# Norm sums and scale of the expert stage worked out in the first block's last weight tiles, and routes of one head with the first token block first

## What is computed

```
h   = rms_norm(x1, norm2_g) * (1 + scale2) + shift2            # 256 x 2048
q   = h @ peer_query            -> per head (8) two halves of 128
s   = q . peer_keys             -> per head and half 128 key scores
top = 16 best of each half; 16 x 16 pair sums; 16 best pairs   # expert = key_a * 128 + key_b
g   = softmax(16 best sums)
out = sum over 8 heads x 16 picks of
      g * gelu(peer_down[expert] . h) * peer_up[expert]        # rows of 2048
x2  = x1 + gt2 * out;  then rms_norm with final_g
```

## Time and profile before

| what | before |
|---|---|
| median of 3 runs | 3666.14 us |
| profiled execution, its own time | 3667.49 us |
| span of its trace | 3665.7 us |
| mean granted TensorE clock | 0.896 of 2.4 GHz |
| TensorE, VectorE, ScalarE, GpSimd busy | 2978.8, 1845.8, 1119.8, 2423.9 us |
| first block's last update ends, first gather, last gather issued at | 999.1, 1075.5, 2411.1 us |

### The profile page before, as it was taken

The page is one execution under the profiler, slowest core; times in us unless marked ns, Lnnn a source line. Parts: engine busy times, 40 slices in busy tenths (PEclk is TensorE's granted clock), DMA queues, the critical chain, the costliest instruction groups (busy, mean ns, idle before and its releaser), DMA issues. The chain is left out here.

```text
span 3665.7 us, 31629 instructions
## 1 busy us (share of the span) xinstructions
PE 2978.8 (81%) x11406; PEld 2100.8 (57%) x11406; DVE 1845.8 (50%) x2199; ACT 1119.8 (31%) x1784; POOL 2423.9 (66%) x1132
## 2 busy tenths in 40 slices
PE   6899999999876665555466676569999998999997
PEld 2677777888753432222122222238888877878876
DVE  1776365423146779998777667751147321121221
ACT  2422355344311111111121111124455444434433
POOL 0444575588724567766778778758767687888875
PEclk7999999999988887776778987779999998999998
DMA  9898643365548899999999999975545455556543
GB/s 390 295 362 314 226 158 121 115 199 191 185 168 362 368 419 427 427 427 427 422 427 427 425 427 425 427 282 184 174 148 185 138 184 183 189 191 201 191 155 142
DMA packets 314642, 1017.91 MB, mean 278 GB/s; under 512 B 21609, under 2 KB 24261, under 8 KB 246653
## 3 DMA queue, kind: packets, MB, share of 16 engines
q1 hardware_dynamic: 234032, 465.09, 36.9%
q0 software_dynamic: 73728, 536.90, 34.8%
q10 hardware_dynamic: 6732, 13.96, 1.2%
HBM read 1011.66 MB, written 4.23 MB: 277 GB/s over the span
## 5 line engine op out<-in xcount | busy, mean ns | idle before, releaser
L1638 PE MATMUL banks<-up_rows,pick_diagonal 128*128 128x512 f32 x1024 | 674.9, 820 | 496.1 <-DMA up_rows<-peer_up,picked_experts 465.4
L654 POOL TENSOR_TENSOR block_weights_lo<-weight_ring,block_weights_hi 128x1024 fp32r<-128x1024 f32 x224 | 552.8, 2478 | 421.4 <-ACT block_weights_hi L647 316.5
L1638 PEld LDWEIGHTS banks<-up_rows,pick_diagonal 128*128 128x128 f32 x1024 | 261.8, 268 | 887.5 <-issue 830.9
L1903 DVE CUSTOM_DVE_ANT_0 down_rows<-down_rows,h_tokens 128x2048 f32<-128x2048 f32 x256 | 585.0, 2291 | 243.9 <-DMA down_rows<-peer_down,picked_experts 235.8
L1565 POOL DMA_INDIRECT up_rows<-peer_up,picked_experts x256 | 472.0, 1844 | 319.8 <-PE banks L1638 165.1
L654 POOL TENSOR_TENSOR merge_weights_lo<-weight_ring,merge_weights_hi 128x1024 fp32r<-128x1024 f32 x208 | 500.4, 2408 | 123.0 <-ACT merge_weights_hi L647 122.9
L1559 POOL DMA_INDIRECT down_rows<-peer_down,picked_experts x256 | 468.2, 1829 | 165.0 <-DVE picked_experts L1843 86.6
L654 POOL TENSOR_TENSOR in_weights_lo<-weight_ring,in_weights_hi 128x1024 fp32r<-128x1024 f32 x176 | 423.6, 2416 | 136.0 <-ACT in_weights_hi L647 135.5
L647 ACT ACTIVATE block_weights_hi<-weight_ring 128x1024 fp32r<-128x1024 f32 x224 | 235.4, 1058 | 423.3 <-PE banks L512 225.4
L1733 ACT ACTIVATE pick_gelu<-pick_dots 128x2 f32<-128x2 f32 x128 | 26.0, 203 | 1067.1 <-DVE pick_dots L1903 1067.1
L1862 DVE SCALAR_TENSOR_TENSOR expert_sum<-up_rows,pick_share,expert_sum 128x2048 f32<-128x2048 f32 x125 | 293.9, 2351 | 79.1 <-ACT pick_share L1736 73.7
(11 more groups left out here) (477 smaller groups left out, 5033.0 us busy)
## 6 DMA issues: line engine op xcount, KB each, us to landing
weight_ring<-w_in SPq DMA_DIRECT2D x232, 1024.0 KB, 5.0
cond_ring<-w_ada SPq DMA_DIRECT2D x128, 512.0 KB, 6.4
weight_ring<-w_ada SPq DMA_DIRECT2D x32, 1024.0 KB, 9.0
weight_ring<-w_out SPq DMA_DIRECT2D x32, 1024.0 KB, 5.0
weight_ring<-peer_query SPq DMA_DIRECT2D x16, 1024.0 KB, 12.2
weight_ring<-w_ret_out SPq DMA_DIRECT2D x8, 1024.0 KB, 5.0
weight_ring<-w_mlstm_out SPq DMA_DIRECT2D x8, 1024.0 KB, 5.1
weight_ring<-w_mem_kv SPq DMA_DIRECT2D x8, 1024.0 KB, 16.1
```

What stands on the lines that cost most here:

```text
L654: pool.tensor_tensor(self.lo[:, at], ring.tile[:, slot, h * self.HALF:(h + 1) * self.HALF], self.hi[:, at], ALU.subtract).then_inc(ring.us ...
L1638: mm = pe.matmul(ps[:, 4 + b], diag[:, G % 2], up[:, p % ROWS, b * CG:(b + 1) * CG], start=(G % PER_TB == 0), stop=(G % PER_TB == PER_TB - ...
L1903: dve.tensor_tensor_reduce(down[:, p % ROWS], down[:, p % ROWS], h2[:, G // PER_TB], 1.0, 0.0, ALU.mult, ALU.add, dots[:, p:p + 1]).then_i ...
```

## The change

1. In the first block SyncE issues, after the tiles of the second `w_out` chunk, twelve loads: scale2 and norm2_g in four pieces each, the keys in two, shift2 in two, into columns of the block's own tensors that are no longer used; the small table is loaded at the block's start. VectorE forms (1 + scale2) * g in four pieces (`scales`) after the first token update, and multiplies the finished columns of x1 by it into `h2` (`scaled`), for chunks 0 to 2 after their update and for chunk 3 in `token_update`. ScalarE sums the squares of the finished columns (`token_squares`, two of 512 wide per chunk) into `e.ss2` and calls Sqrt once before the last of them. In the very last tile TensorE takes both halves for token block 0 before token block 1, and VectorE updates block 0 as soon as that half is done.
2. The expert stage starts with a reduce of `e.ss2`, variance, root and reciprocal. h of each token block is written in four pieces of 512 (times rstd, plus shift2), each with its own count, block 0 first. TensorE turns one fill of keys, block 0's four fills, then does queries and scores of key blocks 0 and 1 for token block 0 alone, then the other key fills and block 1, and so on: `UNITS` is the list of queries, the first four with one token block, the other fourteen (key blocks 2 to 15) with both. Five units are done ahead of the loop, unit 5 + G // 2 in it. The last use of a query chunk is at G = 0, 8, 16, the first of the next at G = 2, 10, 18. ScalarE has the exponential of route 0 between the copies of the keys and those of h of block 1.
3. A route is one head: 16 routes of 16 picks per token block and head, two key lists, one pair list, numbers and normalisation; each takes four groups (`PACE`). The picks of route r are needed at G = 8r.
4. GpSimd waits once for the turned keys before the first up gather.

The core of the diff:

```diff
                         sp.dma_start(x_again(n), tokens_of(io["x"][0])[:, :, n * CG:(n + 1) * CG]).then_inc(late_in, 16)
+                if c == W0 + 1:
+                    sp.wait_ge(m_turned, FILLS)
+                    for n in range(N_OUT):
+                        cols = slice(n * CG, (n + 1) * CG)
+                        sp.dma_start(scale2(n), e.mod_rows[0, 2 * D:3 * D][cols].partition_broadcast(P)).then_inc(early_in, 16)
+                        sp.dma_start(g2(n), io["norm2_g"][0, cols].partition_broadcast(P)).then_inc(early_in, 16)
+                    for j in range(2):
+                        sp.dma_start(early_keys(j), io["peer_keys"][0].rearrange("h a k d -> k (h a) d")[:, j * HP // 2:(j + 1) * HP // 2]).then_inc(early_in, 16)
+                        sp.dma_start(early_shift(j), e.mod_rows[0, D + j * D // 2:D + (j + 1) * D // 2].partition_broadcast(P)).then_inc(early_in, 16)
...
-                    for tb in range(TB):
-                        if first == 0 and h == 0 and g >= 2:
-                            if g - 2 < N_COLS:
...
+            def token_squares(n):
+                if n == 0:
+                    act.wait_ge(m_lo_out, FILLS)
+                for tb in range(TB):
+                    act.wait_ge(out_done, (2 * N_OUT + n) * TB + tb + 1)
+                    act.activation(ps[:, 4 + tb], e.x[:, tb, n * CG:(n + 1) * CG], ACT.Square, accum_out=e.ss2[:, tb, n:n + 1])
...
             def token_update(n):
                 g = Y0 + 2 * N_OUT + n
-                dve.wait_ge(split.free, split.free_after(M0 + tiles_at_end[g]))
                 for tb in range(TB):
+                    if n == N_OUT - 1 and tb == 0:
+                        dve.wait_ge(first_half_done, 1)
+                    else:
+                        dve.wait_ge(split.free, split.free_after(M0 + tiles_at_end[g]))
                     step(dve.tensor_tensor(prod[:, tb], ps[:, 2 * (g % 2) + tb], gt1(n), ALU.mult))
                     dve.tensor_tensor(e.x[:, tb, n * CG:(n + 1) * CG], x_again(n)[:, tb], prod[:, tb], ALU.add).then_inc(out_done, 1)
-                dve.wait_ge(out_done, (2 * N_OUT + n + 1) * TB)
+                    if n == N_OUT - 1:
+                        scaled(n, tb)
+
+            def scaled(n, tb):
+                dve.wait_ge(out_done, (2 * N_OUT + n) * TB + tb + 1)
+                cols = slice(n * CG, (n + 1) * CG)
+                step(dve.tensor_tensor(h2[:, tb, cols], e.x[:, tb, cols], scale2(n), ALU.mult))
+
+            def scales():
+                dve.wait_ge(early_in, 13 * 16)
+                for n in range(N_OUT):
+                    step(dve.scalar_tensor_tensor(scale2(n), scale2(n), 1.0, g2(n), ALU.add, ALU.mult))
...
-        PER_TB, PER_ROUTE = GROUPS // TB, NB // 2 * TOP // 2
-        ROUTES, R_PICKS = GROUPS // PER_ROUTE, NB // 2 * TOP
-        EARLY = 6
+        PER_TB, PER_ROUTE, PACE = GROUPS // TB, TOP // 2, 4
+        ROUTES, R_PICKS = GROUPS // PER_ROUTE, TOP
+        UNITS = [(i, (tb,)) for tb in range(TB) for i in range(2)] + [(i, (0, 1)) for i in range(2, HP)]
+        unit_of = lambda i, tb: 2 * tb + i if i < 2 else i + 2
+        q_count = lambda u: sum(1 for i, _ in UNITS[:u + 1] if i % NB < NB - 1)
+        EARLY = 5
...
+            turn_keys(0, 0)
+            for g in range(H_FILLS):
+                turn_h2(1 + g, 0, g)
+            pe.wait_ge(turned_out, 1 + H_FILLS)
+            for u in range(2):
+                query(u)
+            for u in range(2):
+                score(u)
+            for f in range(1, KEY_FILLS):
+                turn_keys(H_FILLS + f, f)
+            for g in range(H_FILLS):
+                turn_h2(KEYS_TURNED + g, 1, g)
             pe.wait_ge(turned_out, FILLS)
-            for i in range(EARLY):
-                query(i)
-                if 1 <= i < NB:
-                    score(i - 1)
-                if i == NB - 1:
-                    score(i)
-            score(EARLY - 2)
+            for u in range(2, 4):
+                query(u)
+            for u in range(2, 4):
+                score(u)
+            query(4)
+            score(4)
 
             for G in range(GROUPS):
                 p = 2 * G + 1
...
+            for u in range(2, 4):
+                copy_query(u)
+            for u in range(2, 4):
+                copy_score(u)
+            copy_query(4)
+            copy_score(4)
 
             for G in range(GROUPS):
                 first = 2 * G
@@ -1742,15 +1827,12 @@
                     act.wait_ge(odd_added, G - 1)
                 act.activation(diag[:, G % 2], e.ident[:], ACT.Copy, scale=share[:, first + 1:first + 2]).then_inc(diag_ready, 1)
 
-                if G == 0:
...
@@ -1882,18 +1959,17 @@
                 dve.tensor_tensor(e.hT_lo[:, tb, 4 * f:4 * f + 4], ps[:, fill % 2].rearrange("p (a t) -> p a t", a=4),
                                   e.hT_hi[:, 4 * f:4 * f + 4, tb * P:(tb + 1) * P], ALU.subtract).then_inc(lo_out, 1)
 
-            dve.wait_ge(rows_in, 48)
-            step(dve.scalar_tensor_tensor(scale2, scale2, 1.0, g2, ALU.add, ALU.mult))
-            rms_stats_on_vector(dve, step, TB, ss[:], rstd[:], squares, var_ready, root_ready)
+            step(dve.tensor_reduce(ss[:], e.ss2[:], AX, ALU.add))
+            dve.tensor_scalar(rstd[:], ss[:], 1.0 / D, EPS, ALU.mult, ALU.add).then_inc(var_ready, 1)
+            dve.wait_ge(root_ready, 1)
+            step(dve.reciprocal(rstd[:], rstd[:]))
             for tb in range(TB):
-                step(dve.scalar_tensor_tensor(h2[:, tb], e.x[:, tb], rstd[:, tb:tb + 1], scale2, ALU.mult, ALU.mult))
-                dve.tensor_tensor(h2[:, tb], h2[:, tb], shift2, ALU.add).then_inc(h2_ready, 1)
-            dve.wait_ge(h2_ready, TB)
-            for nb in range(NB):
-                key_list(0, nb)
-            for j in range(NB // 2):
-                pair_list(0, j)
-            dve.wait_ge(iota_in, 16)
+                for f in range(H_FILLS):
+                    dve.scalar_tensor_tensor(part(h2[:, tb], f), part(h2[:, tb], f), rstd[:, tb:tb + 1], shift2(f), ALU.mult, ALU.add).then_inc(h2_ready, 1)
+            dve.wait_ge(h2_ready, TB * H_FILLS)
+            for a in range(2):
+                key_list(0, a)
+            pair_list(0)
             pick_numbers(0)
             normalize(0)
 
@@ -1903,18 +1979,16 @@
                     dve.tensor_tensor_reduce(down[:, p % ROWS], down[:, p % ROWS], h2[:, G // PER_TB], 1.0, 0.0, ALU.mult, ALU.add,
                                              dots[:, p:p + 1]).then_inc(dot_done, 1)
 
-                r, at = divmod(G, PER_ROUTE // 2)
+                r, at = divmod(G, PACE)
                 if 1 <= r < ROUTES:
-                    if at < NB // 2:
-                        pair_list(r, at)
+                    if at == 0:
+                        pair_list(r)
+                    if at == 1:
+                        pick_numbers(r)
                     if at == 2:
-                        pick_numbers(r)
-                    if at == 4:
                         normalize(r)
-                if r + 1 < ROUTES:
-                    order = (2, 3, 5, 7) if r == 0 else (3, 5, 6, 7)
-                    if at in order:
-                        key_list(r + 1, order.index(at))
+                if r + 1 < ROUTES and at >= 2:
+                    key_list(r + 1, at - 2)
 
                 if G == TAIL:
                     dve.wait_ge(even_added, PER_TB)
@@ -2783,6 +2857,7 @@
         e.pool_step = Steps(nc.gpsimd, sem("pool_steps"))
         e.act_step = Steps(nc.scalar, sem("act_steps"))
         e.final_rstd, e.x_kept = sb("final_rstd", [P, TB]), sem("x_kept")
+        e.iota16, e.ss2 = sb("iota16", [P, PEER_TOP]), sb("x1_square_sums", [P, TB, D // CG])
 
         e.mod_rows = nc.dram_tensor("mod_rows", (1, 4 * D), F32, kind="Internal").ap()
         e.x_rows = nc.dram_tensor("x_rows", (P, TB, D), F32, kind="Internal").ap()
```

More of the change, by code:

```diff
@@ L908, in states @@
+                    if tb == TB - 1:
+                        mm.then_inc(split.free, 1)
+                    elif last and h == 1:
+                        mm.then_inc(first_half_done, 1)
             def states():
@@ L1830, in pick_numbers, with pair_list @@
+            def pair_list(r):
+                wide = [P, TOP, TOP]
+                step(dve.tensor_tensor(pairs[:], top_now[:, 0].unsqueeze(2).to_broadcast(wide), top_now[:, 1].unsqueeze(1).to_broadcast(wide), ALU.add))
+                top16(dve, step, pairs[:].rearrange("p i j -> p (i j)"), left[:], best, best_at)
+                dve.tensor_tensor(weight[:, r * R_PICKS:(r + 1) * R_PICKS], best[:], best[:, 0:1].to_broadcast([P, TOP]), ALU.subtract).then_inc(shifted, 1)
             def pick_numbers(r):
-                at, flat = best_at[:].rearrange("p h k -> p (h k)"), [P, R_PICKS, TOP]
+                wide = [P, R_PICKS, TOP]
```

244 lines of the change are left out of this document (131 added, 113 removed).

## The result

| | before | changed |
|---|---|---|
| median us (range) | 3667.85 (3663.9 to 3672.56) | 3641.43 (3638.13 to 3641.99) |
| span of the profiled execution | 3665.7 | 3639.8 |
| first gather, last gather issued | 1075.5, 2411.1 | 1027.6, 2387.7 |

What follows compares the result with a forecast made beforehand. DMA was taken to bound the expert stage, from the first gather on. The terms -47.1 + 9.8 + 11.7 + 2 + 3 + 0.5 = -20.1 us gave 3646, range 3629 to 3661; this forecast case had chance 0.66.

Steps and rivals of the forecast that it cites:

- Start, -47.1: Start of the expert stage: first gather at 1028.4 instead of 1075.5, a gain of 47.1 us.
- Second chunk's bytes, +9.8: Gather stage: the second query weight chunk, 4.19 MB at 427 GB/s, is now loaded inside it, costing 9.8 us.
- Third switch, +11.7: Gather stage: a third query chunk switch, at G=2, idles DMA like the two before, 11.7 us, bounds 0 and 15.
- the first idle place: Sign in the gather stage: first of three DMA idle places of 11 to 12 us, 35 to 60 us after first gather.
- Rival A: Gather stage: the new chunk switch costs no idle time, or all clocks are kind; about 3631, chance 0.10.
- Late gelu, +2: Start of expert stage: ScalarE's first gelu is 6 to 13 us late, mostly hidden; 2 us, bounds 0 and 13.
- VectorE, +3: First 64 groups: one-head routes add 0.41 us of VectorE work per group, mostly fitting its waits; 3 us, bounds 0 and 26.
- B: Gather stage: VectorE binds in the first half, 16 to 26 us instead of 3; 3664, chance 0.12.
- C: Groups 0 to 63: VectorE binds and halved operations hardly get shorter; 3683, chance 0.06.
- Rival D: Start of expert stage: an unseen wait eats 20 to 30 us of the earlier start; about 3667, chance 0.06.
- First block, +0.5: First block: added VectorE, ScalarE and load work stays within GpSimd's 4.4 us lead; 0.5 us, bounds 0 and 5.5.
- The lock that was weighed: First block: two-SBUF-input VectorE operations and GpSimd's exclude each other; GpSimd loses up to 6.9 us, sum 2 us worse.

Runs made afterwards that it cites:

- e1: Kernel before with only the second norm's loads, sums and scale moved into the first block: 3647.27 us; first gather 19.0 us earlier.
- e2: Second half of the change alone: kernel before with one-head routes and token block 0 queried first, norm unmoved: 3663.56 us; first gather 25.6 us earlier.
- e3: Changed kernel with all but a sliver of each tile of the second query weight chunk left unloaded: 3622.25 us.
- e9: Changed kernel with the exponential of route 0 put behind ScalarE's copies of block 1's turned tokens: 3642.81 us.
- e6: Changed kernel with one more VectorE operation, result unread, in each of the 64 groups of the gather stage's first half: 3641.83 us.
- e8: Changed kernel with tiles 2 and 3 of query chunks 1 and 3 in separate memory, chunk 1's two loaded before the first gather: 3601.31 us.

## Why the prediction was right

Forecast 3646, measured 3641.43, in the forecast case. By its own steps:

- **Start, -47.1:** measured -47.9. The stage prices held within 1.5 us each; the barrier came a little later than priced (first work at 1000.65), the queries a little sooner, since the first ran partly at the higher clock (0.79 in 1009:1012, 1.00 from 1012) where it was priced wholly at the lower one. e1 and e2 give 19.0 and 25.6, together 3.3 less than both at once.
- **Second chunk's bytes, +9.8:** 4.22 MB more in the stage, 9.9 us. e3 confirms it together with the next term.
- **Third switch, +11.7:** 3 idle places instead of 2; all idle DMA in the stage grew by 14.6. The size was taken from the earlier trace rows, and the changed kernel's own line above has nine empty slices of 1.25, 12.8 us with the partly filled ones. One sign was wrong: the first idle place was to come 35 to 60 us behind the first gather and comes 70 behind it (about 1098), because TensorE's wait for tiles begins at 1069.6 but the gathers issued ahead keep DMA busy for another 28 us. And the prediction's 27 us of idle in the stage before count 2.5 MB that landed after 2425; with 562.09 MB in 1075:2425 they are 33. The forecast doesn't use that figure. Rival A (a switch costs nothing) fell: the slow start doesn't bring the tiles early, because the load can only be issued at 1055, when the slot is free.
- **Late gelu, +2:** at most 2, and by e9 nothing that can be told. The ten rows that can be issued ahead did cover it.
- **VectorE, +3:** about 0. This term was mis-sized. It took the free time from two waits in the stretch where VectorE is fullest and charged it for all 64 groups, while VectorE is busy 73.72 of 100 us in 1180:1280; e6 shows that twice the added work costs nothing measurable. Rivals B and C fell with it, and the 256-wide operations do take 0.43, not 0.69. Rival D fell by the first gather at 1027.6.
- **First block, +0.5:** TensorE never waited on another engine there, 97.09 of 100 us busy. The eight products and the scales took VectorE long, though (below).
- The sum -47.9 + 24.5 - 2.5 = -25.9 is the span's difference, 3665.7 to 3639.8. The missing 5.8 against -20.1: 0.8 at the start; 5.5 priced for late gelu, VectorE and first block, which show next to nothing, less 3.0 by which the idle grew more than priced; and 2.5 behind the last gather, where the prediction had nothing. That tail is 1247.4 to 1254.6 us over all the kernels here, so 2.5 is within its scatter.

Three of the 5.5 us that were priced too high were made up for by idle time priced too low, so the sum came nearer than its terms.

The lock that was weighed (SBUF — State Buffer, Who interferes with whom, in the Trainium skill) shows, but mostly on the other engine. VectorE's groups from 915 to 1000 in the changed kernel (count, busy us, mean ns, idle before), then GpSimd's there, and GpSimd's in the kernel before:

```profile
L1386 DVE TENSOR_TENSOR h_tokens<-x_tokens,lat_cols 128x512 f32<-128x512 f32 x8 | 14.0, 1746 | 0.2
...
L1391 DVE SCALAR_TENSOR_TENSOR lat_cols<-lat_cols 128x512 f32<-128x512 f32 x2 | 5.6, 2777 | 0.1
```

```profile
L654 POOL TENSOR_TENSOR block_weights_lo<-weight_ring,block_weights_hi 128x1024 fp32r<-128x1024 f32 x28 | 71.8, 2583 | 6.5 <-ACT block_weights_hi L647 6.3
```

```profile
L654 POOL TENSOR_TENSOR block_weights_lo<-weight_ring,block_weights_hi 128x1024 fp32r<-128x1024 f32 x28 | 69.0, 2466 | 8.0 <-ACT block_weights_hi L647 8.0
```

Beside GpSimd's splits a 512-wide VectorE operation takes up to 2.8 us instead of 0.69, that is up to about one split of 2.5 us longer. GpSimd's mean is 2583 ns instead of 2466, the mean of the same 28 splits before, so 3.3 us over the stretch, where the rule read against GpSimd made it 6.9 and the prediction 2.1. It stayed within GpSimd's lead, and VectorE had the time. The trace agrees with the lock, but the engine that waits is mostly VectorE, and pricing it as GpSimd's loss overstated it.

## What to carry to other kernels

When work is reordered so that a bandwidth-bound stage starts earlier, ask what falls out of the idle gap into the stage: here 48 us of earlier start brought 26, because a 4 MB load and one more buffer turnover moved in. Where weight loads run beside large-row gathers, count packets: a queue gets its turn, not its bytes, so spread an urgent load over two queues or ask for it earlier, before trimming compute. And an engine that is 93% busy in one window may have time to spare in the rest of the stage: read its busy time window by window, and add work to it in an experiment, before pricing it as the bound.

## What the runs showed that was not expected

- One load queue of 2.0 KB packets beside gathers of 7.3 KB packets got 21% of the bytes (1355 packets against 1357), two queues 36% (368 and 362 against 362). Splitting twelve 1 MB loads over two queues took 25 to 35 us off three different kernels, more than the second half of the change.
- 81 us of added VectorE work cost 28 us, and 27 us of it nothing measurable, because VectorE is 88 to 95% busy only from about 1380 to 1680; from 1100 to 1380, with switches and weight loads in between, it is 74 to 85% busy.
- A TensorE wait of 8.8 us for a weight tile costs nothing in e8; in the changed kernel three in a row, 22.0 us in all, leave about 12 us of DMA idle.
